# The last row tiles of a final LayerNorm loaded late, and the straggling expert tile normed in the middle of them

## The reference, cut to what matters

```python
x = layer_norm(ALPHA * x + mixed, ln1_g[l], ln1_b[l])
x = layer_norm(ALPHA * x + grouped_moe(x, w_router, b_router, w_gate_up, w_down),
               ln2_g[l], ln2_b[l])
```

## Time and profile before

| | us |
|---|---|
| median of three runs | 1188.76 (1186.89 to 1188.95) |
| the profiled execution, its own time | 1186.35 |
| its span in the trace | 1184.2 |
| all xf loads begin (SP, L1311) | 1144.24 |
| last scatter begins (GpSimd, L1401) | 1178.55 |

### The profile page before, as it was taken

One profiled execution on the slowest core, in us unless ns is written; L12 is line 12 of the kernel. 1 busy time (PEld: TensorE's weight loads), 2 busy tenths in 40 slices (PEclk: granted clock), 3 DMA queues, 4 the chain that ended last, 5 costly groups with the idle time before them and its releaser, 6 DMA issues.

```text
span 1184.2 us, 17084 instructions
## 1 busy us (share of the span) xinstructions
PE 1104.6 (93%) x5645; PEld 921.6 (78%) x5646; DVE 817.9 (69%) x1147; ACT 557.6 (47%) x808; POOL 92.4 (8%) x100
## 2 busy tenths in 40 slices
PE   7999999999989989899999999989999999999970
PEld 5888888879777778778788887768788888888750
DVE  5799999835365755566586588788579556548657
ACT  5111211233476755656333033277578545548655
POOL 0000000000000000000000000044111211112220
PEclk9999999999999999999999999899999999999985
DMA  6121332322201010171334235579899866699785
GB/s 254 54 84 50 107 89 89 107 93 68 71 19 41 19 41 1 37 303 53 152 142 160 86 128 218 205 271 380 324 319 381 321 200 200 215 389 326 286 255 205
DMA packets 47862, 199.57 MB, mean 169 GB/s; under 512 B 5184, under 2 KB 5696, under 8 KB 45744
## 3 DMA queue, kind: packets, MB, share of 16 engines
q1 hardware_dynamic: 41600, 176.18, 39.4%
q0 software_dynamic: 6192, 22.48, 7.6%
HBM read 166.20 MB, written 32.51 MB: 168 GB/s over the span
## 4 chain that ended last, share of the span: by engine, by line
PE 76%; DMA 7%; DVE 7%; ACT 6%; issue 4%; DVEq 0%; SPq 0%; ACTq 0%; POOL 0%; POOLq 0%
PE ps L465 17%; PE ps L467 16%; PE ps L466 16%; PE ps L1427 7%; PE ps L1429 7%; PE ps L1428 7%; DMA gu<-in_wexp 5%; PE ps L550 1%; PE ps L1496 1%; PE ps L1423 1%; PE ps L536 1%; ACT pr L797 1%; ACT pth L821 1%; DVE ptl L1039 1%; DMA acc_rows<-ys,to_now 1%
## 5 line engine op out<-in xcount | busy, mean ns | idle before, releaser
L465 PE MATMUL ps<-xh,wh 128*128 128x512 f32 x512 | 203.2, 397 | 12.3 <-DVE xl L901 8.1
L467 PE MATMUL ps<-xh,wl 128*128 128x512 f32 x512 | 200.4, 391 | 0.0
L466 PE MATMUL ps<-xl,wh 128*128 128x512 f32 x512 | 200.3, 391 | 0.0
L1329 DVE TENSOR_TENSOR gu<-gu (+1 forms) x128 | 148.5, 1219 | 35.3 <-issue 23.8
L924 DVE SCALAR_TENSOR_TENSOR cv<-u,dw_t,cv 128x1024 f32<-128x1024 f32 x120 | 154.1, 1284 | 3.7
L1427 PE MATMUL ps<-gu,xgh 128*128 x336 | 133.4, 397 | 3.4 <-DVE xgl L1783 3.4
L1323 ACT ACTIVATE gu<-gu (+1 forms) x128 | 124.5, 1047 | 22.6 <-DMA gu<-in_wexp 14.5
L1429 PE MATMUL ps<-gu,xgl 128*128 x336 | 131.1, 390 | 0.0
L1428 PE MATMUL ps<-gu,xgh 128*128 x336 | 130.8, 389 | 0.0
L465 PEld LDWEIGHTS ps<-xh,wh 128*128 128x128 f32 x512 | 96.8, 189 | 34.4 <-issue 14.5
L467 PEld LDWEIGHTS ps<-xh,wl 128*128 128x128 f32 x512 | 96.7, 189 | 20.7
(11 more groups left out here) (259 smaller groups left out, 2053.0 us busy)
## 6 DMA issues: line engine op xcount, KB each, us to landing
gu<-in_wexp SPq DMA_DIRECT2D x64, 1024.0 KB, 8.8
dn_raw<-in_wexp SPq DMA_DIRECT2D x16, 2048.0 KB, 11.0
raw<-in_wblk SPq DMA_DIRECT2D x52, 512.0 KB, 4.0
gate_cols<-gst SPq DMA_DIRECT2D x16, 512.0 KB, 5.2
xraw<-in_xT SPq DMA_DIRECT2D x8, 512.0 KB, 7.7
gcm<-gate_cols SPq DMA_DIRECT2D x8, 512.0 KB, 7.0
gam<-gate_cols SPq DMA_DIRECT2D x8, 512.0 KB, 15.0
x<-in_x SPq DMA_DIRECT2D x8, 512.0 KB, 5.7
```

The source lines that it names most:

```text
L465: pe.matmul(o, a_h, b_h, start=first, stop=False)
L466: pe.matmul(o, a_h, b_l, start=False, stop=False)
L467: return pe.matmul(o, a_l, b_h, start=False, stop=last)
L1329: eng.tensor_tensor(gu[:, par, k, 1, :], gu[:, par, k, 1, :].bitcast(F32), gu[:, par, k, 0, :], ALU.subtract).then_inc(gu_lo, 1)
```

## The change

- A second index column is made for each tile, `to_late`: the token's row if it is 768 (= 128 * `LATE`, `LATE` = 6) or more, and otherwise (or for an empty slot) a row beyond the bounds. Two linked VectorE instructions, ahead of `slots_ok`.
- `last_rows` is called ahead of the first norm on VectorE, and the order of the nine norms is 0, 1, 2, 3, the last tile's rows, 4, 5, 6, 7 (`ORDER`; `PLACE` is the inverse).
- After `rows_ok` GpSimd writes those rows of `rows_l` whose token is 768 or more back into `acc_dram` (no addition, the others are left out by the bounds check).
- SP loads tiles 0 to 5 as before, waits for that write, and then loads tiles 6 and 7. These loads are on its queue ahead of all eight stores.
- The scatter of `norm_l` over `out` waits for the stores of tiles 0 to 5 alone (`f_out`; those of 6 and 7 count on `late_out`), and leaves out tokens of 768 and more.

```diff
+    LATE = TT - 2
+    ORDER = (*range(4), TT, *range(4, TT))
+    PLACE = {t: n for n, t in enumerate(ORDER)}
...
         sp.wait_ge(y_out, end1 * 16)
-        for t in range(TT):
+        for t in range(LATE):
+            sp.dma_start(xf[:, t, :], acc_dram[P * t:P * t + P, :]).then_inc(row_in[t], 16)
+        sp.wait_ge(y_out, end1 * 16 + 16)
+        for t in range(LATE, TT):
             sp.dma_start(xf[:, t, :], acc_dram[P * t:P * t + P, :]).then_inc(row_in[t], 16)
         for t in range(TT):
-            sp.wait_ge(f_ok, t + 1)
-            sp.dma_start(out[P * t:P * t + P, :], xf[:, t, :]).then_inc(f_out, 16)
-        sp.wait_ge(f_out, 16 * TT)
+            sp.wait_ge(f_ok, PLACE[t] + 1)
+            sp.dma_start(out[P * t:P * t + P, :], xf[:, t, :]).then_inc(f_out if t < LATE else late_out, 16)
+        sp.wait_ge(f_out, 16 * LATE)
+        sp.wait_ge(late_out, 16 * (TT - LATE))
         sp.wait_ge(last_stored, 1)
...
-        pool.wait_ge(f_ok, TT + 1)
-        pool.wait_ge(f_out, 16 * TT)
+        pool.tensor_copy(to_now[:], to_late[:, bass.ds(end1, 1)]).then_inc(toc, 1)
+        pool.wait_ge(toc, end1 + 2)
+        pool.wait_ge(rows_ok, 1)
+        pool.sem_inc(to_set, 1)
+        pool.indirect_dma_start(out=acc_dram, out_offset=bass.IndirectOffsetOnAxis(ap=to_now[:, 0:1], axis=0),
+                                in_=rows_l[:], in_offset=None, bounds_check=SEQ - 1, oob_is_err=False).then_inc(y_out, 16)
+        pool.wait_ge(f_ok, PLACE[TT] + 1)
+        pool.wait_ge(f_out, 16 * LATE)
         pool.sem_inc(id_set, 1)
         pool.indirect_dma_start(out=out, out_offset=bass.IndirectOffsetOnAxis(ap=to_last[:, 0:1], axis=0),
-                                in_=norm_l[:], in_offset=None, bounds_check=SEQ - 1, oob_is_err=False).then_inc(y_out, 16)
-        pool.wait_ge(y_out, total * 16)
+                                in_=norm_l[:], in_offset=None, bounds_check=P * LATE - 1, oob_is_err=False).then_inc(y_out, 16)
+        pool.wait_ge(y_out, total * 16 + 16)
         pool.sem_inc(last_stored, 1)
...
-        for t in range(TT + 1):
-            if t < TT:
-                total_of(t + 1)
-            act.wait_ge(f_nm, t + 1)
+        for n, t in enumerate(ORDER):
+            if n < TT:
+                total_of(ORDER[n + 1])
+            act.wait_ge(f_nm, n + 1)
...
         link(V.tensor_copy(w_slot[:], ps[:, 5, TAB:2 * TAB]))
+        link(V.tensor_scalar(fst, ps[:, 5, 0:TAB], P * LATE + 0.5, 2.0 * SEQ, ALU.is_lt, ALU.mult))
+        link(V.scalar_tensor_tensor(out=to_late[:], in0=ps[:, 5, 0:TAB], scalar=-1.0, in1=fst, op0=ALU.add, op1=ALU.add))
...
         mean(0)
-        for t in range(TT + 1):
-            if t == TT // 2:
-                last_rows()
-            if t < TT:
-                mean(t + 1)
+        mean(1)
+        last_rows()
+        for n, t in enumerate(ORDER):
+            if 0 < n < TT:
+                mean(ORDER[n + 1])
             scale_row(t)
             finish(t)
```

More of the change, by code:

```diff
@@ L217, in encoder_layer @@
         to_now = tiny("to_now", [P, 1], I32)
+        to_late = tiny("to_late", [P, TAB], I32)
         w_slot = tiny("w_slot", [P, TAB])
@@ L1187, in moe @@
     (x1, x1t, hot_a, hot_b, wr_t, ones, rt_a, rt_b, rank_a, rank_b, slot_i, mh, sums, xgh2, xgl2, hot_0, both, upto_t, val, wide, tc, id0, one_i, init_p, wo_add, gu, dn_h, dn_l, dn_raw, xg, xgh, xgl, hb, hbh, hbl, ys,
-     xf, g2_b, b2_b, rows_l, norm_l, ys2, unread, squares, w_last, to_last, cst, eps2, st6, mv, rstd, nmr, wgt, ids_i, id_now, to_i, to_now, w_slot, tab, cum_i, ends_i, rows_i, br_b,
+     xf, g2_b, b2_b, rows_l, norm_l, ys2, unread, squares, w_last, to_last, cst, eps2, st6, mv, rstd, nmr, wgt, ids_i, id_now, to_i, to_now, to_late, w_slot, tab, cum_i, ends_i, rows_i, br_b,
      ps, psf, ident) = (m[k] for k in (
          "x1 x1t hot_a hot_b wr_t ones rt_a rt_b rank_a rank_b slot_i mh sums xgh2 xgl2 hot_0 both upto_t val wide tc id0 one_i init_p wo_add gu dn_h dn_l dn_raw xg xgh xgl hb hbh hbl ys "
-         "xf g2_b b2_b rows_l norm_l ys2 unread squares w_last to_last cst eps2 st6 mv rstd nmr wgt ids_i id_now to_i to_now w_slot tab cum_i ends_i rows_i br_b "
+         "xf g2_b b2_b rows_l norm_l ys2 unread squares w_last to_last cst eps2 st6 mv rstd nmr wgt ids_i id_now to_i to_now to_late w_slot tab cum_i ends_i rows_i br_b "
          "ps psf ident").split())
@@ L1209, in moe @@
     rows_in = sem("rows_in"); rows_ok = sem("rows_ok"); w_set = sem("w_set"); last_stored = sem("last_stored")
-    f_sum = sem("f_sum"); f_tot = sem("f_tot"); f_nm = sem("f_nm"); f_sq = sem("f_sq"); f_sd = sem("f_sd")
+    late_out = sem("late_out"); f_tot = sem("f_tot"); f_nm = sem("f_nm"); f_sq = sem("f_sq"); f_sd = sem("f_sd")
     f_rs = sem("f_rs"); f_g = sem("f_g"); f_ok = sem("f_ok"); f_out = sem("f_out")
@@ L1695, in total_of @@
                 rows = rows_l[:]
-            act.activation(unread[:, t % 2, :], rows, ACT.Copy, accum_out=mv[:, t, 0:1]).then_inc(f_tot, 1)
+            act.activation(unread[:, PLACE[t] % 2, :], rows, ACT.Copy, accum_out=mv[:, t, 0:1]).then_inc(f_tot, 1)
         total_of(0)
-        for t in range(TT + 1):
-            if t < TT:
-                total_of(t + 1)
-            act.wait_ge(f_nm, t + 1)
+        for n, t in enumerate(ORDER):
+            if n < TT:
+                total_of(ORDER[n + 1])
+            act.wait_ge(f_nm, n + 1)
             act.activation(squares[:], xf[:, t, :] if t < TT else rows_l[:], ACT.Square, bias=nmr[:, t:t + 1],
                            accum_out=mv[:, t, 1:2]).then_inc(f_sq, 1)
-            act.wait_ge(f_sq, t + 1)
+            act.wait_ge(f_sq, n + 1)
             act.activation(rstd[:, t:t + 1], mv[:, t, 1:2], ACT.Sqrt, scale=1.0 / D, bias=eps2[:]).then_inc(f_sd, 1)
@@ L1913, in mean @@
         def mean(t):
-            dve.wait_ge(f_tot, t + 1)
+            dve.wait_ge(f_tot, PLACE[t] + 1)
             dve.tensor_scalar(nmr[:, t:t + 1], mv[:, t, 0:1], -1.0 / D, None, ALU.mult).then_inc(f_nm, 1)
         def scale_row(t):
-            dve.wait_ge(f_nm, t + 1)
+            dve.wait_ge(f_nm, PLACE[t] + 1)
             if t < TT:
-                dve.wait_ge(f_sq, t + 1)
+                dve.wait_ge(f_sq, PLACE[t] + 1)
             dve.scalar_tensor_tensor(out=xf[:, t, :] if t < TT else norm_l[:], in0=xf[:, t, :] if t < TT else rows_l[:],
@@ L1926, in finish @@
             rows = xf[:, t, :] if t < TT else norm_l[:]
-            dve.wait_ge(f_sd, t + 1)
+            dve.wait_ge(f_sd, PLACE[t] + 1)
             dve.reciprocal(rstd[:, t:t + 1], rstd[:, t:t + 1]).then_inc(f_rs, 1)
-            dve.wait_ge(f_rs, t + 1)
-            dve.wait_ge(f_g, t + 1)
+            dve.wait_ge(f_rs, PLACE[t] + 1)
+            dve.wait_ge(f_g, PLACE[t] + 1)
             dve.scalar_tensor_tensor(out=rows, in0=rows, scalar=rstd[:, t:t + 1], in1=b2_b[:],
```

## The result

| | median, us (runs) | kernel before, same job | ratio | 95% interval |
|---|---|---|---|---|
| changed kernel | 1190.85 (12) | 1186.83 | 1.0033 | 1.0023 to 1.0042 |

The change makes the kernel slower by 0.33%, 4.0 us. The time lies in the stated range (1186.0 to 1192.0), but the likeliest case, no change (0.70), was wrong; "slower by over 0.2%" had 0.18. That range had been laid around the median of three runs, 1188.8, and the twelve runs of the same kernel beside the changed one gave 1186.83. The profiled execution took 1188.49 us, its span is 1186.7, 2.5 above the one before, and it is one of the quick ones among the twelve.

A forecast was written before the change was run, and what follows sets the result against it. The prediction took the end to stay with GpSimd's last scatter and its drain. Tail -0.43 us and table +0.47 us summed to 0.0 on a median of 1188.76, so 1188.8 us was forecast, range 1186.0 to 1192.0.

The forecast's parts named there:

- no change: Whole kernel: time within 0.2% (2.4 us) of the kernel before; given 0.70.
- slower by over 0.2%: Whole kernel: more than 2.4 us slower than before; given 0.18.
- When the last tile's rows can be had: Second LayerNorm: the gather lands no sooner, 9.1 us after its start, so `last_rows` starts at 1154.2.
- Rival 2: Second LayerNorm: gather lands before TensorE ends, `last_rows` starts at 1152.9; 2.2 us faster, perhaps 3; chance 0.12.
- VectorE's tail: Nine norms behind `last_rows`: blocks of 2.65 us without a gap, VectorE ending at 1179.29, 1.7 us later than before.
- The new write and the late loads: GpSimd's write into the accumulator lands at 1159.8, tile 6 at 1163.1 with 4 to 5 us of slack; cost zero.
- Rival 1: VectorE's norms hold the issue of GpSimd's new write, and the last scatter: 2.4 to 5 us slower; chance 0.18.
- The last scatter: Kernel's end: starts 0.93 us after store 5 lands (1177.62), end at 1183.3; -0.93 us, -0.43 with 0.5 for interference.
- The table: Two linked VectorE instructions of 32 columns ahead of `slots_ok`: +0.47 us passed to the end, bounds 0 and 0.5.
- The sum: Whole kernel: -0.43 for the tail and +0.47 for the table, 0.0 us in all.
- GpSimd's drain stayed the last thing: Kernel's end: a sign that GpSimd's drain after the last scatter, not SP's branch, still ends the kernel.
- The range: Whole kernel: 1186.0 to 1192.0 us for 8 in 10, taking in the near half of two rivals.

The follow-up runs named there:

- experiment 4: Kernel before with `last_rows` called ahead of the first norm on VectorE, nothing else changed: 1188.23 us, ratio 1.0014 to the kernel before.
- experiment 1: Changed kernel with 16 one-column memsets on GpSimd between the gather of the last tile's rows and the index copy: 1186.23 us, ratio 0.9999 to the kernel before.
- 6: Changed kernel with the 16 memsets, and tile 0 scaled and finished ahead of `last_rows`: 1185.27 us, ratio 0.9984 to the kernel before.
- experiment 7: Changed kernel with 16 memsets, tile 0 finished ahead of `last_rows`, and only the one needed index column, made late, replacing the table: 1183.45 us, ratio 0.9964.
- 2: Kernel before with 7 one-column memsets on GpSimd ahead of its wait for the eight stores: 1188.25 us, ratio 1.0015 to the kernel before.
- 5: Kernel before with 16 one-column memsets on GpSimd ahead of its wait for the eight stores: 1186.67 us, ratio 1.0001 to the kernel before.
- 8: As experiment 7, with three tiles loaded after the write and the last scatter waiting for five stores: 1182.77 us, ratio 0.9965 to the kernel before.

## Why the prediction was right or wrong

**When the last tile's rows can be had: right.** I said 1154.2 and a gather as long as before. It took 9.1 us again (1145.36 to 1154.49 in the chain), with six loads as with eight, and `last_rows` started at 1154.59. The 0.4 us are mostly the later start of the loads. Over the ten profiles the gather took 8.2 to 9.2 us, with five, six or eight loads alike, so the start of `last_rows` is only known to about 1 us, and the 0.4 owes something to luck. Rival 2, the early gather, did not occur. By the Trainium skill ("DMA: Bandwidth & Descriptors", section "SWDGE vs HWDGE vs iDMA") the software and hardware queues alternate; an alternation from the first descriptor showed here no more than before, since the gather's first packets came 5.0 us after its issue began (4.5 before).

**VectorE's tail: right.** Blocks of 2.65 us, end at 1179.59 where 1179.3 stood; alone (experiment 4) the early `last_rows` costs 1.7 us by the ratio (0.4 to 3.0), as worked out, and 1.05 in the trace.

**The new write and the late loads: right.** SP went on at 1159.68 (1159.8), the sum of tile 6 was not held up. Rival 1, VectorE holding the issue, is refuted here: amid VectorE's norms the write's issue took 1.20 us, and the last scatter's 1.14 to 1.16 in experiments 1, 6 and 7. (The last one's 0.97 in the changed kernel says nothing on this: VectorE had ended at 1179.59.) The prediction took the rule on the shared port (the Trainium skill, "SBUF — State Buffer", section "Who interferes with whom"), that a VectorE instruction with two SBUF inputs contends with a GpSimd instruction that reads SBUF, as a strict lock on the whole issue, which would have made it long; these rows show no such lock. What made two issues 6 and 9 us long in the middle of the kernel (again 6.29 and 9.09 after) was not tried.

**The last scatter: wrong, and this is the step that failed.** "It starts 0.93 after 1176.69, at 1177.62", with at most 1.7 for VectorE and 0.4 for store 7. Store 5 landed at 1177.0, but the scatter started at 1181.03, 4.0 us later and not 0.93. The prediction named no cost for GpSimd's own program there, and so put it at nothing. The trace shows 3.69 us without a releaser and an 8 KB packet of instructions inside. That it is the loading of GpSimd's program, which the added instructions had shifted so that the edge of a piece falls between the wait and the scatter, is shown by moving that edge alone: away in the changed kernel (1, minus 4.6 us), onto the same place in the kernel before (2, plus 1.8), and past it (5, nothing). With the code loaded early, the changed kernel comes out at 0.9999, the zero that my sum gave. The single terms add up to rather more: the table 1.5 for 0.47, and the tail 39.28 against 39.72 to 39.98 in the three profiles with the old order and no gap, thus -0.4 to -0.7 for -0.43. Their +0.8 to +1.1 also lies in the interval (up to 1.0011, 1.3 us), so the runs don't tell it from zero. GpSimd's drain stayed the last thing, as forecast, in experiments 1, 6, 7 and 8 too.

**The table: the term was too small.** 0.47 us by the rows of its like; 0.8 at the `dn_raw` load, of which 0.36 is the longer stand ahead of `gu`, and 1.5 (0.1 to 2.9) on the whole. What makes that stand longer is open, and so is the rest up to 1.5.

**The sum.** In the profiled executions: table and expert phase +0.3 (the first load at 1144.56 for 1144.24), tail 42.12 - 39.98 = +2.1, together the 2.5 of the spans. On the medians 4.0 is made up of the code loading (4.6 by the medians of experiment 1, 2.8 in the trace's tail), the table (1.5), and the reordering's own gain (0.7 in the trace: 39.28 against 39.98). With the one figure for the loading this gives 5.4, with the other 3.6; each ratio is uncertain by about 1.2 us, and the 4.0 lies between. That the profiled execution shows less than the median is in part its short expert phase; whether the loading takes longer without a profiler could not be seen.

**The range.** That 1190.85 lies in it is luck in part. Its upper end, 1192.0, stood 3.2 us above the 1188.8 taken for the kernel before, and the change was 4.0 us; a start from 1186.83 would have put the measured time outside. The upper part of the range also stood for rival 1, which did not occur, and not for the loading of a program.

## What to carry to other kernels

A step that is to run at once when a long wait ends must have its code there: a few added instructions anywhere ahead on that engine's queue can move the edge of a piece of program into the critical place, and a gap with no releaser with an "instruction" packet inside it is its mark. Moving the edge with idle instructions inside an earlier wait is a cheap test, and the cure; the count matters, since 16 closed the gap and 7 opened it. Work that must wait for late data belongs behind what is ready already on an engine that runs in order (one norm put ahead of `last_rows` gave 2.7 us in the trace), and a column that only the last tile needs is better made in an idle place than in a chain that many engines wait for. The best version here (experiment 7) takes 1183.45 us, by the ratio 0.36% less than the kernel before.

## What the runs showed of the hardware that I had not expected

- An 8 KB piece of GpSimd's program, needed on the spot, made the way to the scatter 3.2 us instead of 0.93 with the DMA queues empty (experiment 2), and 4.0 us beside two stores (changed kernel). The packet itself is one of 8 KB.
- With two more short instructions ahead of VectorE's register reads, the reads took as long as before (2.72 us), but VectorE stood 0.40 us instead of 0.05 between them and the next large instruction: the same in four profiles, and absent in the six without the two.
- GpSimd's drain at the end of the program takes 2.03 to 2.11 us after its last transfer has landed, whereas SP's takes 7 ns; in experiment 1 GpSimd's drain began 1.4 us ahead of SP's (1186.0 and 1187.4) and still ended last. It was seen in every profile and not varied.
